# Overlapping the chunks of a conformer/attention residual block: the next chunk's input norm, GLU, q/k/v, convolution and its norm run inside this chunk's back half

## The chip, the cores and the metric

The kernel runs on one core of a Trainium2 chip. The metric is device time in microseconds for one launch, the median over several runs. All times below are microseconds unless they are marked ns.

## What is computed

One encoder layer over a stream of 2048 tokens with 1024 features, everything in float32:

```python
u = rms_norm(h, g_pre_mix); z = u @ w_in          # -> GLU input | q | k | v | branch gates
c = a * sigmoid(b)                                # a, b: the two halves of the GLU input
c = causal_depthwise_conv(c, conv_dw_w, conv_dw_b)    # 31 taps, 512 channels
c = silu(layer_norm(c)); y_conv = c @ w_conv_out
y_attn = sliding_window_sink_attention(rope(q), rope(k), v) @ w_attn_out   # 128-token window
h = h + rms_norm((sig(gA)*y_conv + sig(gB)*y_attn) @ w_out, g_post_mix)
gate, val = split(rms_norm(h, g_pre_ffn) @ w_up)  # 2 x 2816
gate = causal_depthwise_conv(gate, 3 taps)
h = h + rms_norm((gelu(gate) * val) @ w_down, g_post_ffn)
h = h + (p @ w_ple) * sigmoid(h @ w_ple_gate)
```

## The kernel before

The 2048 tokens are worked off in four chunks of 512 (chunk 0 to chunk 3). Features lie on the partitions, in tiles of 128 features by 512 tokens. Every operand of a large product is split into a high and a low part, and each 128x128 weight tile meets a 512-token tile in three matmuls (hi·hi, hi·lo, lo·hi). The weights are a stream of 122 blocks a chunk; a block holds 8 weight tiles, so it is 24 matmuls. Three slots hold blocks: SyncE loads block n as soon as block n-3 is done. In chunk 0 a block comes as float32 (0.5 MB), ScalarE and GpSimd split it, and both parts (1 MB) are stored to memory; in chunks 1 to 3 the two parts are loaded (1 MB).

Each engine runs one program, written out by hand; semaphores tie them together, and what stands first in an engine's program runs first. A chunk goes through these stages:

1. x is loaded and turned to feature-major by 32 TensorE transposes (L741); its norm gives `u_hi`, `u_lo`. This starts when the chunk ahead has ended.
2. GLU (8 blocks), then q and k with their rotation (`rope`, 5 blocks), then v as 96 matmuls of 128 columns (L760 to L762). VectorE runs the 31 x 4 taps of the convolution (L1069) during these and during attention.
3. Attention in four steps, each with two blocks of gate A between its small matmuls.
4. The layer norm of the convolution (mean L834, squares, `token_sums` L724, `spread` L731, which broadcasts a norm's factor over the partitions), and the merge of both branches (16 blocks).
5. `w_out` (8 blocks): `out_projection` on ScalarE squares and copies each result tile out of PSUM (L367, L524). Then the norm of its result (POST), the residual, and the pre-FFN norm (PRE), whose factor is not applied to `y_hi`/`y_lo` but later, to the up-projection's results (`r_ffn`).
6. The feed-forward in two parts: 16 tiles up (32 blocks), down (16 blocks); 6 tiles up (12), down (6). The first matmuls run four result banks at a time, and two more blocks go to banks 4 and 5 before a bank must be free again.
7. The norm of the feed-forward (PF) is taken while TensorE runs the `w_ple` blocks (2). Then `w_ple_gate` (8 blocks) needs `h3_hi`/`h3_lo`, the tiles of h after the residual; the result is turned back and stored.

A norm over the features is a chain: the last square (ScalarE), its sum (VectorE), `token_sums` (TensorE), the root (ScalarE), six small steps and `diag` (VectorE), `spread` (TensorE).

Of the kernel before, what the change touches and what calls it, by code (L numbers as in the profile page):

```python
# [15 lines left out]
P = 128  # L29
# [12 lines left out]
TAPS_A, TAPS_B = 6, 10  # L42
# [7 lines left out]
F1 = 16  # L50
F2 = NF - F1
# [12 lines left out]
B_UP1 = B_WO + KD_  # L64
B_DN1 = B_UP1 + 2 * F1
B_UP2 = B_DN1 + 2 * KD_
B_DN2 = B_UP2 + 2 * F2
B_WP = B_DN2 + F2 * KD_ // 8
B_PG = B_WP + NP * KD_ // 8
NB = B_PG + KD_  # L70
assert NB == 122 and all(b % 2 == 0 for b in (B_QKV, B_GA, B_MRG, B_WO, B_UP1, B_DN1, B_UP2, B_DN2, B_WP, B_PG, NB))
# [16 lines left out]
N_X, N_LN, N_POST, N_PRE, N_PF = range(5)  # L88
NORMS = 5
Q_LN, Q_POST, Q_PRE, Q_PF = 0, NC, NC + KD_, NC + 2 * KD_  # L90
NQ = NC + 3 * KD_

# [9 lines left out]
def build_kernel(nc, x, p, positions, weights, columns, identity, split_weights, out):  # L102
    with ExitStack() as ctx:
# [1342 lines left out]
```

## Time and profile before

| | us |
|---|---|
| median of 3 runs | 3052.93 (3051.05 to 3054.32) |
| the profiled execution, its own time | 3054.54 |
| its span, first to last instruction | 3052.7 |
| TensorE busy in the span | 2903.9 (95%) |
| VectorE busy | 1564.0 (51%) |
| ScalarE busy | 920.4 (30%) |
| mean granted share of the TensorE clock | 0.973 |

The profiled execution lies 1.6 above the median; the span is 1.8 short of its own time. TensorE's matmuls are pipelined, so its 95% says only that it seldom stands still; how dense the work is has to be read from the distance between matmul starts. The chunks' `w_out` stages start at 325.72, 1087.78, 1825.24 and 2562.93.

### The profile page before, as it was taken

The numbers are of one execution on the slowest core, as the hardware profiler recorded it, in microseconds if no ns is written. First come the engines' busy times: TensorE is split into PE (matmuls) and PEld (weight loads), VectorE is DVE, ScalarE is ACT, GpSimd is POOL, SyncE is SP. The second block draws the span as 40 slices with busy tenths as digits, with TensorE's granted clock in tenths as the row PEclk, the third lists the DMA queues.
The fourth block names the chain that finished last, engine by engine and source line by source line (L and its number), as shares of the span: only waits on it lengthen the run. The fifth ranks groups of instructions, "written<-read, shape, count | busy, mean of one in ns | idle before, by whom it ended". The sixth has DMA issues, their size and how long they took to land.

```text
span 3052.7 us, 33514 instructions
## 1 busy us (share of the span) xinstructions
PE 2903.9 (95%) x13232; PEld 2401.6 (79%) x13232; DVE 1564.0 (51%) x2535; ACT 920.4 (30%) x1661; POOL 299.7 (10%) x126
## 2 busy tenths in 40 slices
PE   6888899999899999999999999999999999899998
PEld 5776778887788778888878887888887878788887
DVE  6894477325778426412458834540356862542035
ACT  3463343333426223111233522210123541311013
POOL 2223334444200000000000000000000000000000
PEclk8799999999999999999999999999999999999999
DMA  5445757877743454555454344455555345455555
GB/s 208 172 164 215 284 213 289 290 285 280 262 167 137 158 184 176 194 194 189 184 207 171 133 179 176 183 193 194 189 189 208 142 151 195 160 193 193 193 193 179
DMA packets 180925, 600.37 MB, mean 197 GB/s; under 512 B 18336, under 2 KB 37024, under 8 KB 180768
## 3 DMA queue, kind: packets, MB, share of 16 engines
q1 hardware_dynamic: 163872, 589.83, 53.0%
q10 hardware_dynamic: 16896, 8.39, 0.9%
q8 instruction: 105, 1.72, 0.2%
q14 instruction: 52, 0.43, 0.0%
HBM read 461.84 MB, written 136.31 MB: 196 GB/s over the span
## 4 chain that ended last, share of the span: by engine, by line
PE 79%; DVE 15%; ACT 3%; issue 2%; DMA 1%; POOL 0%; ACTq 0%; POOLq 0%; SPq 0%; DVEq 0%
PE ps L690 22%; PE ps L691 21%; PE ps L692 21%; DVE conv_acc L1069 7%; PE ps L711 4%; PE ps L712 4%; PE ps L715 4%; PE ps L731 1%; DVE prob L1151 1%; DVE s_max L1130 0%; POOL w_lo L318 0%; DVE ca_lo L1162 0%; DVE y_tmp L1205 0%; PE ps L724 0%; DVE h L1042 0%
## 5 line engine op out<-in xcount | busy, mean ns | idle before, releaser
L690 PE MATMUL ps<-y_hi,w_hi 128*128 128x512 f32 x1536 | 602.9, 392 | 7.8 <-POOL w_lo L318 5.2
L692 PE MATMUL ps<-y_hi,w_lo 128*128 128x512 f32 x1536 | 598.9, 390 | 0.0
L691 PE MATMUL ps<-y_lo,w_hi 128*128 128x512 f32 x1536 | 598.8, 390 | 0.0
L1069 DVE SCALAR_TENSOR_TENSOR conv_acc<-conv_in,col,conv_acc 128x512 f32<-128x512 f32 x480 | 350.9, 803 | 0.8
L318 POOL TENSOR_TENSOR w_lo<-w_stage,w_hi 128x1024 fp32r<-128x1024 f32 x122 | 299.5, 2456 | 515.5 <-ACT w_hi L356 515.5
L690 PEld LDWEIGHTS ps<-y_hi,w_hi 128*128 128x128 f32 x1536 | 289.1, 188 | 71.3 <-DVE f_val L1262 4.3
L692 PEld LDWEIGHTS ps<-y_hi,w_lo 128*128 128x128 f32 x1536 | 289.0, 188 | 60.6
L691 PEld LDWEIGHTS ps<-y_lo,w_hi 128*128 128x128 f32 x1536 | 289.2, 188 | 59.9 <-issue 1.0
L690 PE MATMUL ps<-u_hi,w_hi 128*128 128x512 f32 x800 | 320.9, 401 | 0.4 <-POOL w_lo L318 0.4
L691 PE MATMUL ps<-u_lo,w_hi 128*128 128x512 f32 x800 | 313.5, 392 | 0.0
L692 PE MATMUL ps<-u_hi,w_lo 128*128 128x512 f32 x800 | 313.4, 392 | 0.0
L690 PE MATMUL ps<-f_hi,w_hi 128*128 128x512 f32 x768 | 301.5, 393 | 2.2 <-DVE f_lo L1283 2.2
L691 PE MATMUL ps<-f_lo,w_hi 128*128 128x512 f32 x768 | 299.5, 390 | 0.0
L692 PE MATMUL ps<-f_hi,w_lo 128*128 128x512 f32 x768 | 299.5, 390 | 0.0
L356 ACT ACTIVATE w_hi<-w_stage 128x1024 fp32r<-128x1024 f32 x122 | 129.1, 1059 | 267.2 <-PE ps L692 214.4
L1293 DVE TENSOR_TENSOR f_lo<-ps,f_hi 128x512 fp32r<-128x512 f32 x8 | 5.2, 686 | 339.9 <-ACT f_hi L597 339.9
L690 PEld LDWEIGHTS ps<-u_hi,w_hi 128*128 128x128 f32 x800 | 152.0, 190 | 34.1 <-issue 3.4
L691 PEld LDWEIGHTS ps<-u_lo,w_hi 128*128 128x128 f32 x800 | 151.9, 190 | 33.5 <-issue 3.0
L692 PEld LDWEIGHTS ps<-u_hi,w_lo 128*128 128x128 f32 x800 | 151.5, 189 | 32.1
L711 PE MATMUL ps<-y_hi,w_hi 128*128 128x512 f32 x384 | 154.5, 402 | 17.8 <-ACT y_hi L548 9.9
L690 PEld LDWEIGHTS ps<-f_hi,w_hi 128*128 128x128 f32 x768 | 144.6, 188 | 33.4 <-DVE f_lo L1283 2.6
L691 PEld LDWEIGHTS ps<-f_lo,w_hi 128*128 128x128 f32 x768 | 144.5, 188 | 30.6 <-issue 1.0
(179 smaller groups left out, 3991.9 us busy)
## 6 DMA issues: line engine op xcount, KB each, us to landing
w_hi<-split_weights SPq DMA_DIRECT2D x366, 512.0 KB, 3.2
w_lo<-split_weights SPq DMA_DIRECT2D x366, 512.0 KB, 4.2
w_stage<-in_weights SPq DMA_DIRECT2D x122, 512.0 KB, 4.3
split_weights<-w_hi SPq DMA_DIRECT2D x122, 512.0 KB, 2.6
split_weights<-w_lo SPq DMA_DIRECT2D x122, 512.0 KB, 3.9
x_rows<-in_x SPq DMA_DIRECT2D x5, 2048.0 KB, 10.2
out_h<-ple ACTq DMA_DIRECT2D x32, 256.0 KB, 5.2
p_rows<-in_p SPq DMA_DIRECT2D x4, 512.0 KB, 5.9
```

Source lines behind the costliest of these rows:

```text
L318: nc.gpsimd.tensor_tensor(w_lo[:, b % SLOTS], w_stage[:, b % SLOTS], w_hi[:, b % SLOTS].bitcast(F32), ALU.subtract).then_inc(w_lo_ready, 1)
L356: copy(w_hi[:, b % SLOTS], w_stage[:, b % SLOTS], ACT.Copy).then_inc(w_hi_ready, 1)
L690: nc.tensor.matmul(bank, w_hi[:, slot, kk], hi, start=start, stop=False)
L691: nc.tensor.matmul(bank, w_hi[:, slot, kk], lo, start=False, stop=False)
L692: return nc.tensor.matmul(bank, w_lo[:, slot, kk], hi, start=False, stop=stop)
L711: nc.tensor.matmul(ps[:, banks[o]], w_hi[:, slot, first + o], hi[:, k], start=(k == 0), stop=False)
L712: nc.tensor.matmul(ps[:, banks[o]], w_lo[:, slot, first + o], hi[:, k], start=False, stop=False)
L715: last = nc.tensor.matmul(ps[:, banks[o]], w_hi[:, slot, first + o], lo[:, k], start=False, stop=(k == 7))
L731: nc.tensor.matmul(ps[:, BC], ones[:, :], diag[:, :, :].rearrange("p t n -> p (t n)"), start=True, stop=True).then_inc(bc_ready, 1)
L1069: V.scalar_tensor_tensor(dst, src, column("conv_w", t + j * TAPS), dst, ALU.mult, ALU.add).then_inc(conv_tap, 1)
L1151: V.tensor_tensor(prob[:, s], prob[:, s], s_rec[:, s].unsqueeze(2).broadcast_to([P, PAIRS, P]), ALU.mult).then_inc(pn_ready, 1)
L1293: V.tensor_tensor(f_lo[:, F1 - NP + k], ps[:, PV + k], f_hi[:, F1 - NP + k].bitcast(F32), ALU.subtract).then_inc(p_lo, 1)
```

## The change

The order of the blocks across chunks is now a list that all engines read:

```python
order = [(0, b) for b in range(B_GLU, B_GA)]
for c in range(CHUNKS):
    order += [(c, b) for b in range(B_GA, B_UP[0])]
    if c + 1 < CHUNKS:
        order += [(c + 1, b) for b in range(B_GLU, B_QKV)]
    order += [(c, b) for b in range(B_UP[0], B_WP)]
    if c + 1 < CHUNKS:
        order += [(c + 1, b) for b in range(B_QKV, B_GA)]
    order += [(c, B_PG + j) for j in range(4)]
    order += [(c, b) for b in (B_WP, B_PG + 4, B_PG + 5, B_WP + 1, B_PG + 6, B_PG + 7)]
```

So chunk c+1's GLU (8 blocks) stands between chunk c's `w_out` and its up-projection, and chunk c+1's q, k, v (6 blocks) between chunk c's last down-projection and its `w_ple_gate`. The 122 blocks a chunk are the same ones. With them move:

- x is loaded twice: `rows_u` (four loads of 0.5 MB, issued before block 2 of `w_out`) is scaled row by row by its norm and turned for `u_hi`/`u_lo`; `rows_h` (2 MB, issued before block 3 of `w_out`) is turned for h. Both turnings stand inside `w_out`'s blocks 4 to 7, 16 tiles in all, through banks 0 and 2, so that block 4 first waits until `out_projection` has emptied these two.
- v is a whole block of 24 matmuls like the others, followed by four transposes.
- The taps of the next chunk's convolution stand in VectorE's program in groups of two inside the up-projection's tiles (42 of them in each of the first two parts), and 40 more beside the first down-projection.
- The feed-forward has three blocks of 8, 8 and 6 tiles; the PRE factor is applied to the input (`u2_tile`), not to the results; the conv over the gate reads PSUM.
- Output tiles are turned back and stored in the next chunk's attention.
- The layer norm of the next chunk's convolution stands between the `w_ple_gate` blocks.

TensorE's program after `w_out` (condensed; `more` is false in chunk 3, where all `c + 1` parts drop out):

```diff
+                if more:
+                    pe.wait_ge(y2_out, c * KD_ + 6)
+                    glu_pair(c + 1, 0, between=lambda: token_sums(POST, c))
+                    spread(POST, c)
+                    glu_pair(c + 1, 1)
+                    glu_pair(c + 1, 2)
+                    token_sums(PRE, c)
+                    glu_pair(c + 1, 3, between=lambda: spread(PRE, c))
+                else:
+                    token_sums(POST, c)
+                    spread(POST, c)
+                    token_sums(PRE, c)
+                    spread(PRE, c)
+                by_tile(c, B_UP[0], UP_BANK[0] + UP_BANK[1], y_hi, y_lo, u2_hi, u2_lo, c * KD_)
+                for t in range(2, FB[1]):
+                    up(c, t)                      # waits ft_ready >= c * NF + t - 1
...
+                down(c, 2)
+                if more:
+                    full_block(c + 1, B_QKV, QK_BANK[0], u_hi, u_lo)
+                token_sums(PF, c)
+                if more:
+                    full_block(c + 1, B_QKV + 1, QK_BANK[1], u_hi, u_lo)
+                spread(PF, c)
+                if more:
+                    for j in range(2, PAIRS + 1):
+                        full_block(c + 1, B_QKV + j, QK_BANK[j], u_hi, u_lo)
+                    full_block(c + 1, B_QKV + PAIRS + 1, V_BANK, u_hi, u_lo)
+                    pe.wait_ge(rope_done, (c + 1) * (PAIRS + 1) + 4)
+                by_tile(c, B_PG, PG_BANK[0:4], y_hi, y_lo, h3_hi, h3_lo, c * KD_,
+                        between=(lambda: value_rows(c + 1)) if more else None)
+                ple_tiles(c, 0)
+                if more:
+                    conv_mean(c + 1)
+                ple_gate(c, 4)
+                if more:
+                    token_sums(LN, c + 1)
+                ple_gate(c, 5)
+                if more:
+                    spread(LN, c + 1)
+                ple_tiles(c, 4)                   # tile j waits ple_mul of tile j - 2
```

On VectorE, at the place after the norm PF, the program before has this (h_tmp and h are the residual, y_lo the low part that `w_ple_gate` needs):

```order
L1227 TENSOR_TENSOR h<-h,h_tmp 128x512
L1320 TENSOR_TENSOR y_lo<-h,y_hi 128x512
L1222 SCALAR_TENSOR_TENSOR h_tmp<-acc,col,ps 128x512
L1227 TENSOR_TENSOR h<-h,h_tmp 128x512
L1320 TENSOR_TENSOR y_lo<-h,y_hi 128x512
L1222 SCALAR_TENSOR_TENSOR h_tmp<-acc,col,ps 128x512
L1227 TENSOR_TENSOR h<-h,h_tmp 128x512
```

The changed program has the rotation of the next chunk's q (rope_a, rope_b, qT) among them:

```order
L1365 SCALAR_TENSOR_TENSOR h_tmp<-acc,col,ps 128x512
L1370 TENSOR_TENSOR h<-h,h_tmp 128x512
L1365 SCALAR_TENSOR_TENSOR h_tmp<-acc,col,ps 128x512
L1370 TENSOR_TENSOR h<-h,h_tmp 128x512
L1431 TENSOR_TENSOR y_lo<-h,y_hi 128x512
L1246 TENSOR_TENSOR rope_a<-ps,cos_t 128x512
L1247 TENSOR_TENSOR rope_b<-rope_b,sin_t 128x512
L1250 TENSOR_TENSOR qT<-rope_a,rope_b 128x512
L1431 TENSOR_TENSOR y_lo<-h,y_hi 128x512
```

This group of nine stands three times in a row, once for each of the q tiles 1 to 3; what moved in are the three rotation steps.

On ScalarE, at the same place, the program before makes the copies y_hi one after the other:

```order
L342 ACT_TABLE_LOAD
L342 ACTIVATE n_root<-ps,col 128x4
L615 ACTIVATE ple<-ps 128x512 x6
L619 ACTIVATE y_hi<-h 128x512 x8
L629 ACTIVATE ple<-ps 128x512 x2
```

The changed program has the swapping copies of the rotation (four of 32 partitions for each q or k tile) between them:

```order
L430 ACT_TABLE_LOAD
L430 ACTIVATE n_root<-ps,col 128x4
L471 ACTIVATE rope_b<-ps 32x512 x4
L597 ACTIVATE y_hi<-h 128x512 x3
L471 ACTIVATE rope_b<-ps 32x512 x4
L597 ACTIVATE y_hi<-h 128x512 x2
L471 ACTIVATE rope_b<-ps 32x512 x4
```

Each swap now stands behind a y_hi copy that waits for VectorE's residual, and VectorE's rope_a waits for the swap.

On VectorE, around the squares of the layer norm, before:

```order
L1179 SCALAR_TENSOR_TENSOR conv_acc<-ps,conv_acc 128x512 x4
L1030 MEMSET ssum 128x512
L1036 TENSOR_TENSOR ssum<-ssum,sq 128x512 x4
L987 TENSOR_SCALAR n_var<-ps 128x4
L988 RECIPROCAL n_r<-n_root 128x4
```

and in the changed program, between `w_ple_gate`'s blocks:

```order
L1324 SCALAR_TENSOR_TENSOR conv_acc<-ps,conv_acc 128x512 x4
L1153 MEMSET ssum 128x512
L1442 TENSOR_TENSOR ple_t<-ps,ple_sg 128x512
L1444 TENSOR_TENSOR h<-h,ple_t 128x512
L1442 TENSOR_TENSOR ple_t<-ps,ple_sg 128x512
L1444 TENSOR_TENSOR h<-h,ple_t 128x512
L1160 TENSOR_TENSOR ssum<-ssum,sq 128x512 x4
```

Two tiles of the per-layer embedding (`ple_add`) now stand between the centring and the sums of the squares.

## Rows read from the trace of the kernel before

**Rows 1.** The page, busy time by engine: us, share, instructions.

```profile
PE 2903.9 (95%) x13232; PEld 2401.6 (79%) x13232; DVE 1564.0 (51%) x2535; ACT 920.4 (30%) x1661; POOL 299.7 (10%) x126
```

**Rows 2.** Windows: stretch, length, busy and count by engine, clock, DMA share, GB/s.

```profile
1320.85:1407.90 87.05, 87.05 (x386) 72.03 (x384) 2.08 (x3) 5.46 (x9) 0.00 (x0) 1.00 0.53 193
...
325.72:1087.78 762.06, 727.00 (x3309) 598.98 (x3308) 447.06 (x628) 279.73 (x465) 200.94 (x83) 0.98 0.65 234
1087.78:1825.24 737.46, 716.84 (x3308) 593.83 (x3307) 351.15 (x628) 197.94 (x382) 0.00 (x0) 0.99 0.50 181
2562.93:3052.74 489.81, 471.19 (x2087) 387.62 (x2085) 182.36 (x322) 106.58 (x168) 0.00 (x0) 0.98 0.51 186
```

**Rows 3.** Windows, as above: places in chunk 1 where TensorE is less dense.

```profile
914.45:925.12 10.67, 10.67 (x98) 10.67 (x96) 8.59 (x13) 3.97 (x8) 0.00 (x0) 1.00 0.27 100
990.70:1022.38 31.68, 26.57 (x111) 20.51 (x110) 21.81 (x40) 11.02 (x19) 0.00 (x0) 0.95 0.32 117
1109.54:1142.15 32.61, 25.02 (x107) 19.33 (x106) 10.01 (x20) 10.78 (x20) 0.00 (x0) 0.91 0.51 185
1510.81:1521.36 10.55, 8.77 (x41) 6.75 (x40) 5.07 (x13) 4.08 (x9) 0.00 (x0) 1.00 0.36 125
1566.79:1579.32 12.53, 6.97 (x52) 5.44 (x50) 9.30 (x20) 7.42 (x13) 0.00 (x0) 0.90 0.61 184
...
1142.15:1146.66 4.51, 4.51 (x11) 3.54 (x12) 4.51 (x8) 1.95 (x4) 0.00 (x0) 0.50 0.01 4
1142.15:1320.85 178.70, 178.41 (x778) 146.96 (x779) 89.38 (x161) 43.28 (x64) 0.00 (x0) 0.99 0.50 183
```

**Rows 4.** Timeline, norm POST of chunk 1: start, length, engine, instruction, idle before.

```profile
1132.18 0.69 DVE L1036 TENSOR_TENSOR ssum<-ssum,sq 128x512 f32<-128x512 f32 x1 [4.58 <-ACT sq L367]
1133.02 1.02 PE L724 MATMUL ps<-ones,ssum 128*128 128x1 f32 x8 [1.56 <-DVE ssum L1036]
1134.13 1.28 ACT L342 ACT_TABLE_LOAD   x1 [1.54 <-PE ps L724]
1135.42 0.26 ACT L342 ACTIVATE n_root<-ps,col 128x4 f32<-128x4 f32 x1
...
1137.61 2.07 PE L731 MATMUL ps<-diag,ones 128*128 128x512 f32 x2 [3.56 <-DVE diag L998]
...
1139.72 0.75 DVE L1222 SCALAR_TENSOR_TENSOR h_tmp<-acc,col,ps 128x512 f32<-128x512 f32 x1 [1.62 <-PE ps L731]
1140.50 0.69 DVE L1227 TENSOR_TENSOR h<-h,h_tmp 128x512 f32<-128x512 f32 x1
...
1141.29 0.72 ACT L548 ACTIVATE y_hi<-h,col 128x512 fp32r<-128x512 f32 x1 [5.60 <-DVE h L1227]
...
1142.15 0.77 PE L711 MATMUL ps<-y_hi,w_hi 128*128 128x512 f32 x1 [2.47 <-ACT y_hi L548]
```

**Rows 5.** Timeline, ScalarE: out-projection tiles 0 and 1 of chunk 1.

```profile
1110.23 0.60 ACT L367 ACTIVATE sq<-ps 128x512 f32<-128x512 f32 x1 [15.93 <-PE ps L715]
...
1111.68 0.62 ACT L524 ACTIVATE acc<-ps 128x512 f32<-128x512 f32 x1
```

**Rows 6.** Window, as in Rows 2: x and weights loaded together.

```profile
1550.00:1562.00 12.00, 12.00 (x62) 10.11 (x62) 5.67 (x9) 3.26 (x6) 0.00 (x0) 1.00 0.99 370
```

**Rows 7.** Groups by line, VectorE: instruction, count, busy, mean ns, idle before.

```profile
L1069 DVE SCALAR_TENSOR_TENSOR conv_acc<-conv_in,col,conv_acc 128x512 f32<-128x512 f32 x480 | 350.9, 803 | 0.8
```

**Rows 8.** Timeline, ScalarE and VectorE: one rotation in chunk 1.

```profile
909.26 2.40 ACT L409 ACTIVATE rope_b<-ps 32x512 f32<-32x512 f32 x4 [3.04 <-PE ps L692]
...
910.24 0.68 DVE L1101 TENSOR_TENSOR rope_a<-ps,cos_t 128x512 f32<-128x512 f32 x1
...
911.55 0.69 DVE L1105 TENSOR_TENSOR qT<-rope_a,rope_b 128x512 f32<-128x512 f32 x1
```

**Rows 9.** Timeline, VectorE: layer norm of chunk 1.

```profile
1004.08 2.48 DVE L1179 SCALAR_TENSOR_TENSOR conv_acc<-ps,conv_acc 128x512 f32<-128x512 f32 x4 [1.62 <-PE ps L834]
...
1007.14 1.52 DVE L1036 TENSOR_TENSOR ssum<-ssum,sq 128x512 f32<-128x512 f32 x2
```

More of the change, by code:

```diff
@@ new lines, in gate_b_tile, with centred_squares, silu @@
+            def gate_b_tile(c, j):
+                done(c, GB_BLOCK[j])
+                if j >= 2:
+                    act.wait_ge(merged, c * KD_ + j - 1)
+                copy(gate_b[:, j % 2], ps[:, GB_BANK[j % 2]], ACT.Sigmoid).then_inc(gate_b_ready, 1)
+            def centred_squares(c, first, end):
+                for j in range(first, end):
+                    act.wait_ge(ln_centred, c * NC + j + 1)
+                    square(LN, c, j, conv_acc[:, j], j % 2)
+            def silu(c, first, end):
+                for j in range(first, end):
@@ new lines, in product, with full_block @@
+            def product(bank, c, b, kk, hi, lo, start, stop):
+                slot = PLACE[c, b] % SLOTS
+                nc.tensor.matmul(bank, w_hi[:, slot, kk], hi, start=start, stop=False)
+                nc.tensor.matmul(bank, w_hi[:, slot, kk], lo, start=False, stop=False)
+                return nc.tensor.matmul(bank, w_lo[:, slot, kk], hi, start=False, stop=stop)
+            def full_block(c, b, bank, hi, lo, between=None):
+                ready(c, b)
+                for k in range(8):
+                    if k == 4 and between is not None:
+                        between()
+                    last = product(ps[:, bank], c, b, k, hi[:, k], lo[:, k], k == 0, k == 7)
+                last.then_inc(block_done, 1)
@@ new lines, in token_sums, with spread @@
+            def token_sums(kind, c):
+                pe.wait_ge(ss_added, c * NQ + Q_AT[kind] + (NC if kind == LN else KD_) + 2)
+                for t in range(TT):
+                    last = nc.tensor.matmul(ps[:, SMALL, t:t + 1], ssum[:, P * t:P * t + P], ones[:, 0:1],
+                                            start=True, stop=True)
+                last.then_inc(ssum_done, 1)
+            def spread(kind, c):
+                pe.wait_ge(diag_ready, c * 4 + kind + 1)
+                nc.tensor.matmul(ps[:, BC], ones[:, :], diag[:, :, :].rearrange("p t n -> p (t n)"),
+                                 start=True, stop=True).then_inc(bc_ready, 1)
@@ L967, in _ @@
+                ple_gate(c, 7)
+                if not more:
+                    for f in range(2, KD_):
+                        out_tile(c, f, 6 + f % 2)
         @block.vector
@@ new lines, in add_down, with h3_tile @@
+            def add_down(c, q, j):
+                if q == 1:
+                    dve.wait_ge(dn_first, c * KD_ + j + 1)
+                else:
+                    dve.wait_ge(dn_acc, c * 2 * KD_ + j + 1)
+                done(c, dn_done(q, j))
+                V.tensor_tensor(acc[:, j], acc[:, j], ps[:, dn_bank(q, j)], ALU.add).then_inc(dn_acc, 1)
+            def h3_tile(c, j):
+                if j >= 2:
+                    dve.wait_ge(h3_mid, c * KD_ + j - 1)
+                normed(c, j, "g_post_ffn", h3_step)
+                residual(c, j, h3_step, h3_mid)
```

2042 lines of the change are left out of this document (1098 added, 944 removed).

## Prediction

> **What bounds the kernel now.** The page's busy times come first [rows 1]: TensorE 95%, VectorE 51%, ScalarE 30%. TensorE sets the end, so I read the rest as one question: how much of its time is not dense matmul? The densest stretch gives the unit. 384 matmuls of the first down-projection take 87.05 [rows 2], 0.2267 each, so a block of 24 is 5.44. A chunk's 122 blocks are 663.8. A steady chunk, from one `w_out` to the next, takes 737.5 [rows 2]: 73.7 is something else. Chunk 0 (weights split on the fly) takes 762.1 for the same stretch, and the last one has 489.8 from `w_out` to the end. The windows then show where the 73.7 lies [rows 3]: v's 96 small matmuls take 10.67 for what a block does in 5.44; the layer norm's stretch holds four blocks (21.8) and lasts 31.7; the stretch of the norm POST again holds four blocks and lasts 32.6; the norm PF's holds 30 matmuls (6.8) and lasts 10.6; the chunk boundary holds only transposes and a broadcast and lasts 12.5.
>
> The timeline [rows 4] shows what such a gap is: the last sum at 1132.18, `token_sums`, table load 1.28, root and `diag` to 1137.61, then residual and copy, and TensorE starts again at 1142.15. It starts slow: for the next 4.51 the granted clock is 0.50 [rows 3], the 1.2 GHz level, and some ten matmuls run where twenty would at 2.4 GHz. So this gap costs about 2.2 more than its length.
>
> **What goes, in a steady chunk.** v as a block and four transposes: 10.67 - 5.44 - 0.4 = 4.8. The boundary: 12.5, plus 2.1 for the slow start, less 1.6 for four output tiles that only move: 13.0. Layer norm: 31.7 - 21.8 = 9.9, of which its sums and broadcasts (2.1) stay: 7.8. POST: 32.6 - 21.8 = 10.8; the stretch behind it, with PRE's sums and factor, holds 768 matmuls (174.1) in 178.7 [rows 3], 4.6 more; 15.4 in all, of which four small steps, 2.9, stay: 12.5. PF: 10.6 - 6.8 - 1.4 = 2.3. Together **40.4**.
>
> **What comes, in a steady chunk.** Most of the moved work is covered: for taps, six at 0.66 to 0.80 [rows 7] plus some 3.5 of its own is under the 10.9 that TensorE needs for an up tile. But I walked the order of each engine and found places where TensorE catches up.
> - *Turning x twice.* 16 tiles where there were 8, and they now cut into blocks. A tile's four transposes are about 0.4 and a break 0.05: 7.1.
> - *Banks 0 and 2.* `w_out` block 4 waits until two result tiles are squared and copied: from 1109.54, the end of the four-bank part, to 1112.3 [rows 5]: 2.8.
> - *Loads.* From the end of the merge, x (2 + 2 MB) goes ahead of `w_out`'s block 3. With blocks 2 and 3 that is 6.3e6 bytes; at the 370 GB/s of a full queue [rows 6] 17 plus a latency of about 2 gives 19, and block 3 is wanted after three blocks, 16.3. I take 3; bounds 0 and 8.
> - *Third up tile.* Before, two blocks went to banks 4 and 5 here. Now `up(2)` waits for tile 0's `f_tmp`: tap on ScalarE 0.6, two on VectorE 0.75 each, two conv taps 1.3, product 0.7, hand-overs: 4.5, plus 2.1: 6.6. Without cover nothing else hides it. Bounds 3.5 and 7.
> - *Rotation before `w_ple_gate`.* TensorE needs rotations 0 to 3 done. A group of nine VectorE instructions waits in its middle: two residual tiles 2.8 (pitch 1.39, from 0.78 and 0.61 [rows 4]), ScalarE's copy of the second 0.65, its swap 2.40 [rows 8], then rope 1.95 and a low part 0.6: 8.5, where VectorE's own work is 6.0. From the broadcast of PF: 1.06 + first tile and rotation 3.9 + two groups 17 + the third up to its rotation 8.0 = 29.9; TensorE has the broadcast 0.55 and four blocks 21.8, that is 22.3. Wait 7.6, plus 2.1: 9.7. Bounds 0 (VectorE never waits for the swaps) and 11.
> - *Layer norm's sums.* One block covers centring 2.6 (with 0.9 to start), zeroing 0.5, two embedding tiles 2.8, and four sums that alternate with squares 3.0 [rows 9]: 9.6 against 5.4. Wait 4.1, plus 2.1: 6.2. Bounds 2 and 7.
> - *Embedding tiles 6 and 7.* Tile 6 waits for scaling 2.6 and a product; tile 7 for two silus, a table load 1.28 and a sigmoid on ScalarE: 1.3 + 1.4 = 2.7. Bounds 0 and 5.
>
> Together **38.1**. A steady chunk changes by -2.3.
>
> The Trainium skill has a rule against this change: a switch of the activation table is a load of about 1283 ns and a drain, about 2.66 us together (ScalarE: Activation LUTs, What ACT_TABLE_LOAD costs). The changed kernel alternates sigmoid, silu and root between the `w_ple_gate` blocks. In the trace the load is 1.28 and the root starts 0.01 later, so no drain is seen; by the skill's figure tile 7 would wait 1.4 longer in each of three chunks, and the sum would be 4 higher.
>
> **The first chunk.** Up to `w_out` I expect nothing. The taps bind there: VectorE's 62 or so [rows 7] times 0.8 and more between GLU and scores, so v's shorter time is not the end's; and ScalarE splits three weight blocks before it copies the first tile of x. Bounds -5 and +4. From there to chunk 1's `w_out`: -2.3, its longer boundary gone too (4), but the x loads meet 1.5 MB of weight traffic a block, and block 3's split comes after them: +8. So +2; bounds -6 and +10.
>
> **The last chunk** has no next chunk to cover anything. Banks 2.8, h's eight tiles 3.6. POST and PRE stand bare: the chain to the first sum 2.5, 3.3 from sums to broadcast (4.6 in rows 4 less the table load, which runs ahead now), 2.1 to VectorE, then eight tiles of normed, residual and sum, 0.66 + 0.6 + 0.6 and a start, 16.4; sums to broadcast 3.3; tile and copy 3.2; with ends 31.0, slow start 2.2. That is 33.2 against the 15.4 of now: 17.8. Third up tile 5.8. PF: 9.5 + 2.1 against 3.9: 7.7. The tail 0.5. Together **38.2**.
>
> **Sum.** 0 + 2 - 2 x 2.3 + 38.2 = +35.6 on the profiled execution's own 3054.5, so 3090; the median of before lies 1.6 lower, and I round down a little, to **3086**, since the 2.1 of a slow start need not follow a wait as short as some of these. Dropping the slow starts at the new waits takes 22 away, the loads 9, the first chunk 9 more at its low bound; loads at 8 and the first chunk at its high bound add 25. Range 3054 to 3112.
>
> **Rivals.**
> 1. *The hand-overs don't bind* (faster). If VectorE keeps its own pace between residual and rotation and between centring and squares, the group of nine is 6.0, rotations end at 34 just with TensorE, the layer norm's wait shrinks to what its own sums need and the embedding tiles are free: 18.6 less in each of three chunks, 3086 - 56 = 3030. It decides from some 13 saved a chunk. For it: VectorE is only half busy, and an out-of-step copy can be done early. Against it: ScalarE runs its list in order, and the swap stands behind a copy that waits. Chance 0.12.
> 2. *The loads starve TensorE*: 4 MB of x at the worst place; if a wait of 8 with a slow start follows in chunks 1 and 2 and 20 in chunk 0, +26: 3112. For it: the queue is at 0.99 with 2 MB [rows 6]. Against it: steady chunks load at half of what it can. Chance 0.15.
> 3. *It cancels*: my forecast with no slow starts after new waits and cheaper loads, 3050 to 3058. Chance 0.13.
> The forecast itself, 3058 to 3104: 0.60.
>
> A measurement of this kernel tells about 0.2%, 6, from no change. Faster by more: rival 1 and a little of 3, 0.13. Within: 0.09. Slower: 0.78.
>
> **What would show it.** `w_out` to `w_out` in the steady chunks 733 to 738, and 525 to 532 from the last `w_out` to the end. TensorE waits of 7 to 8 before `w_ple_gate` on the rotation, 4 to 5 before the third up tile on the product, 4 before the layer norm's sums, and one of some 20 in the last chunk before the PRE sums. If steady chunks take under 725, rival 1 holds and the forecast is wrong; if `w_out`'s blocks 2 and 3 wait over 5 for weights, rival 2.

## The result and the profile after

The changed kernel takes 3161.9 (3159.15 to 3165.26, four runs) against 3053.62 of the kernel before (3051.05 to 3055.86, four runs): the ratio is 1.0355, interval 1.0337 to 1.0373. That is 108 slower, where 33 was forecast, and outside the range.

The page of the changed kernel has TensorE and ScalarE busy within 7 of [rows 1], VectorE 154 less, and a span that is 105 longer:

```profile
span 3157.3 us, 32749 instructions
...
PE 2910.3 (92%) x13080; PEld 2397.9 (76%) x13080; DVE 1410.4 (45%) x2392; ACT 917.1 (29%) x1635; POOL 322.9 (10%) x126
```

So the 105 are not more work: they are waits, and matmuls at a lower clock (the mean granted clock is 0.963 in this execution, 0.973 before). GpSimd's 322.9 for the same 126 instructions, against 299.7, points to one of the causes; I come to it below. The windows, cut at the start of each chunk's `w_out` (length, busy of PE, PEld, DVE, ACT and POOL, clock, DMA share, GB/s), say where the waits are. They answer to [rows 2]:

```profile
0.00:328.44 328.44, 256.46 (x1152) 211.58 (x1153) 213.97 (x315) 141.46 (x267) 101.90 (x43) 0.93 0.54 194
328.44:1147.45 819.01, 732.28 (x3272) 602.06 (x3271) 389.66 (x596) 281.12 (x462) 221.03 (x83) 0.95 0.61 221
1147.45:1887.82 740.37, 718.57 (x3272) 594.70 (x3270) 324.27 (x596) 199.51 (x379) 0.00 (x0) 0.98 0.50 183
1887.82:2627.62 739.80, 718.14 (x3272) 593.84 (x3270) 324.29 (x596) 199.52 (x379) 0.00 (x0) 0.98 0.50 183
2627.62:3157.34 529.72, 484.89 (x2119) 395.74 (x2117) 158.20 (x289) 95.53 (x149) 0.00 (x0) 0.95 0.47 172
```

| stretch | before | after | difference | forecast |
|---|---|---|---|---|
| start to `w_out` of chunk 0 | 325.7 | 328.4 | +2.7 | 0 |
| to `w_out` of chunk 1 | 762.1 | 819.0 | +56.9 | +2 |
| to `w_out` of chunk 2 | 737.5 | 740.4 | +2.9 | -2.3 |
| to `w_out` of chunk 3 | 737.7 | 739.8 | +2.1 | -2.3 |
| to the end | 489.8 | 529.7 | +39.9 | +38.2 |

The last chunk is as forecast, the steady ones are 5 dearer each, and the first is wrong by 55. TensorE's chain of waits over that stretch (line, what it waited for: total, times, longest) names the reason:

```profile
PE ps L741 <- POOL w_lo L403: 41.0, 6, 20.5
PE ps L765 <- POOL w_lo L403: 16.0, 4, 7.5
PE ps L765 <- issue: 13.4, 1, 13.4
PE ps L741 <- DVE f_tmp L1408: 5.8, 1, 5.8
```

57.0 are waits for GpSimd's `w_lo`, the low part of a weight block that is split in chunk 0 only. The same view of the kernel before has 6.0, 0.8 of them in `w_out` and these:

```profile
PE ps L690 <- POOL w_lo L318: 5.2, 3, 2.3
```

The 13.4 "issue" is in part of the same kind: ScalarE's split for the first `w_ple_gate` block starts at 903.87, behind its copies, and GpSimd's part ends just before TensorE starts at 907.42.

The steady chunk shows the hand-overs that the prediction walked through, one by one:

```profile
PE ps L765 <- DVE qT L1250: 7.4, 1, 7.4
PE ps L741 <- DVE f_tmp L1408: 4.0, 1, 4.0
PE ps L778 <- DVE ssum L1160: 3.3, 1, 3.3
PE ps L765 <- DMA w_lo<-split_weights: 3.0, 1, 3.0
PE ps L741 <- issue: 2.2, 1, 2.2
PE ps L741 <- DVE ple_t L1442: 1.8, 2, 1.1
```

So there are three questions. Why does GpSimd come late in chunk 0, although its own work is unchanged? Do the steady waits cost what the forecast put on them, and can they go? And does the overlap pay when they are gone?

**The longest wait, 20.5.** The timelines of GpSimd and of VectorE around it (start, length, engine, instruction, idle before):

```profile
562.82 23.49 POOL L403 TENSOR_TENSOR w_lo<-w_stage,w_hi 128x1024 fp32r<-128x1024 f32 x2 [14.35 <-ACT w_hi L422]
```

```profile
555.20 26.58 DVE L1208 SCALAR_TENSOR_TENSOR conv_acc<-conv_in,col,conv_acc 128x512 f32<-128x512 f32 x40
```

```profile
584.13 0.76 PE L741 MATMUL ps<-f_hi,w_hi 128*128 128x512 f32 x1 [20.46 <-POOL w_lo L403]
```

Two splits take 23.49. The view by tile (count: shortest, median and longest in ns) gives the longer of them:

```profile
L403 POOL TENSOR_TENSOR w_lo<-w_stage,w_hi x5: 2355/2387/21167, 546.1 to 597.8; 128x1024 fp32r<-128x1024 f32 x5
```

One split takes 21.2 and the others 2.4. The long one begins while the 40 taps run, which fill 555.20 to 581.78 with no gap between two, and ends 2.2 behind the last of them: about the 2.4 that a split takes alone. So it stood for the rest of the row, 19.0, and then ran. No weight is missing; SyncE can't store the block, and so can't load the next, before this split is done. It goes the other way too, for one instruction at a time: here a VectorE step of a kind that takes 0.43 beside it takes 2.55, from just behind GpSimd's start to just behind its end.

```profile
542.58 2.34 POOL L403 TENSOR_TENSOR w_lo<-w_stage,w_hi 128x1024 fp32r<-128x1024 f32 x1 [4.39 <-ACT w_hi L422]
542.65 2.55 DVE L1182 TENSOR_SCALAR angle<-angle,col 128x512 f32<-128x512 f32 x1
```

The Trainium skill has the rule for this (SBUF — State Buffer, Who interferes with whom): VectorE and GpSimd share a pair of ports as an exclusive lock, held for a whole instruction, and a VectorE instruction with two inputs in SBUF contends with a GpSimd instruction that reads SBUF. A tap has two such inputs. The two rows above show the whole-instruction lock, but their VectorE step has only one tensor as input. The kernel before shows it with two inputs; in its steady chunk this product takes 0.69:

```profile
505.06 2.40 POOL L318 TENSOR_TENSOR w_lo<-w_stage,w_hi 128x1024 fp32r<-128x1024 f32 x1 [3.05 <-ACT w_hi L356]
505.60 2.40 DVE L1281 TENSOR_TENSOR f_tmp<-g_act,f_val 128x512 f32<-128x512 f32 x1 [0.99 <-ACT g_act L576]
```

By the rule as it stands a split waits for one tap, 0.66; here it waits for what is left of a row of them. My prediction didn't weigh this rule.

A row of taps need not do that, though. At the start of chunk 0 the same trace has a row of 28, and five splits arrive in it:

```profile
62.11 29.33 DVE L1208 SCALAR_TENSOR_TENSOR conv_acc<-conv_in,col,conv_acc 128x512 f32<-128x512 f32 x28
```

```profile
L403 POOL TENSOR_TENSOR w_lo<-w_stage,w_hi x5: 2406/2481/2987, 64.3 to 85.8; 128x1024 fp32r<-128x1024 f32 x5
```

None takes over 3.0, as the rule has it. These 28 taps alternate between two tiles of `conv_acc`, and each waits for the last but one; the 40 go round four tiles. A row of 16 over four tiles in the kernel before shows both cases, and it was there to be read before the prediction:

```profile
213.73 12.79 DVE L1069 SCALAR_TENSOR_TENSOR conv_acc<-conv_in,col,conv_acc 128x512 f32<-128x512 f32 x16
```

```profile
214.51 2.85 POOL L318 TENSOR_TENSOR w_lo<-w_stage,w_hi 128x1024 fp32r<-128x1024 f32 x1 [2.67 <-ACT w_hi L356]
223.68 5.04 POOL L318 TENSOR_TENSOR w_lo<-w_stage,w_hi 128x1024 fp32r<-128x1024 f32 x1 [6.32 <-ACT w_hi L356]
```

The split that comes 0.8 behind the row's start gets in; the one that comes 10 behind it ends 2.2 after the row's last tap (226.52). What decides between the two cases no run here tests.

### The profile page after: what moved, and what is told of

It reads as the page before. It is cut to its first block, busy times and chain, and to the rows that moved or that the text cites. A ratio compares the mean times of both kernels' runs of the same rounds, so it can differ in the third digit from the quotient of the medians.

```text
span 3157.3 us, 32749 instructions
## 1 busy us (share of the span) xinstructions
PE 2910.3 (92%) x13080; PEld 2397.9 (76%) x13080; DVE 1410.4 (45%) x2392; ACT 917.1 (29%) x1635; POOL 322.9 (10%) x126
## 4 chain that ended last, share of the span: by engine, by line
PE 78%; DVE 5%; DMA 2%; ACT 2%; POOL 1%; issue 1%; SPq 0%; DVEq 0%; ACTq 0%
PE ps L741 21%; PE ps L742 21%; PE ps L743 21%; PE ps L765 4%; PE ps L766 4%; PE ps L769 3%; POOL w_lo L403 1%; DMA w_stage<-in_weights 1%; PE ps L790 1%; DMA w_lo<-split_weights 1%; PE ps L876 1%; ACT rope_b L471 1%; DVE h L1370 1%; DVE h_tmp L1365 1%; PE ps L778 1%
## 5 line engine op out<-in xcount | busy, mean ns | idle before, releaser
L741 PE MATMUL ps<-y_hi,w_hi 128*128 128x512 f32 x1536 | 612.5, 399 | 31.4 <-DVE f_tmp L1408 17.8
L403 POOL TENSOR_TENSOR w_lo<-w_stage,w_hi 128x1024 fp32r<-128x1024 f32 x122 | 322.7, 2649 | 660.4 <-ACT w_hi L422 660.4
L1208 DVE SCALAR_TENSOR_TENSOR conv_acc<-conv_in,col,conv_acc 128x512 f32<-128x512 f32 x480 | 387.1, 865 | 0.1
L741 PEld LDWEIGHTS ps<-y_hi,w_hi 128*128 128x128 f32 x1536 | 293.6, 191 | 96.5 <-DVE f_tmp L1408 19.5
L741 PE MATMUL ps<-u_hi,w_hi 128*128 128x512 f32 x704 | 280.5, 398 | 4.1 <-POOL w_lo L403 4.1
L743 PE MATMUL ps<-u_hi,w_lo 128*128 128x512 f32 x704 | 275.6, 391 | 0.0
L742 PE MATMUL ps<-u_lo,w_hi 128*128 128x512 f32 x704 | 275.3, 391 | 0.0
L1398 DVE SCALAR_TENSOR_TENSOR g_conv<-ps,col,g_conv 128x511 f32<-128x511 f32 x88 | 65.9, 749 | 388.8 <-ACT g_conv L583 388.6
L765 PE MATMUL ps<-y_hi,w_hi 128*128 128x512 f32 x384 | 159.7, 416 | 53.7 <-POOL w_lo L403 16.0
L743 PEld LDWEIGHTS ps<-f_hi,w_lo 128*128 128x128 f32 x768 | 146.1, 190 | 31.0
L741 PEld LDWEIGHTS ps<-u_hi,w_hi 128*128 128x128 f32 x704 | 133.3, 189 | 33.6 <-issue 5.4
L1421 DVE TENSOR_TENSOR acc<-acc,ps 128x512 f32<-128x512 f32 x64 | 43.9, 687 | 257.0 <-PE ps L743 257.0
```

What stands on the lines that cost most here:

```text
L403: nc.gpsimd.tensor_tensor(w_lo[:, slot], w_stage[:, slot], w_hi[:, slot].bitcast(F32), ALU.subtract).then_inc(w_lo_ready, 1)
L741: nc.tensor.matmul(bank, w_hi[:, slot, kk], hi, start=start, stop=False)
L742: nc.tensor.matmul(bank, w_hi[:, slot, kk], lo, start=False, stop=False)
L743: return nc.tensor.matmul(bank, w_lo[:, slot, kk], hi, start=False, stop=stop)
L765: nc.tensor.matmul(ps[:, banks[o]], w_hi[:, slot, first + o], hi[:, k], start=(k == 0), stop=False)
L1208: V.scalar_tensor_tensor(dst, src, column("conv_w", t + j * TAPS), dst, ALU.mult, ALU.add).then_inc(conv_tap, 1)
```

## Experiments

The stretches of each kernel, from its profiled execution, cut as above; medians and ratios beside them. The kernel before ran beside each group: 3051.04 with e1 to e4, 3052.39 with e5 to e8, 3053.0 with e9 to e11, 3053.45 with e12. A stretch comes from one execution and carries some 3 of its own: one that the edit doesn't touch reads 736.9 for 739.8 (e2, chunk 2 to 3) and 532.9 for 529.7 (e6, the last). In e2's case block 3's load is waited for twice, at most 2.0 each, where the change has one wait of 2.6, and the granted clock is 0.99 for 0.98.

| kernel | chunk 0 to 1 | 1 to 2 | 2 to 3 | 3 to end | median | ratio, interval |
|---|---|---|---|---|---|---|
| the change | 819.0 | 740.4 | 739.8 | 529.7 | 3161.9 | 1.0355, 1.0337 to 1.0373 |
| e1 breaks | 802.2 | 740.4 | 740.7 | 531.2 | 3145.11 | 1.0309, 1.0286 to 1.0332 |
| e2 taps later | 805.6 | 740.5 | 736.9 | 531.5 | 3148.06 | 1.0315, 1.0293 to 1.0338 |
| e3 columns | 799.0 | 736.9 | 740.6 | 528.8 | 3129.76 | 1.0253, 1.0225 to 1.0281 |
| e4 swap first | 812.3 | 730.0 | 727.5 | 531.3 | 3136.65 | 1.0281, 1.0266 to 1.0296 |
| e5 split first | 808.9 | 740.4 | 739.8 | 529.7 | 3150.92 | 1.0326, 1.0311 to 1.0341 |
| e6 squares first | 820.7 | 735.2 | 733.8 | 532.9 | 3153.4 | 1.0332, 1.0315 to 1.035 |
| e7 banks | 819.3 | 733.4 | 733.9 | 524.7 | 3144.14 | 1.0303, 1.0288 to 1.0319 |
| e8 load order | 822.1 | 732.7 | 734.5 | 531.5 | 3154.24 | 1.0337, 1.0321 to 1.0352 |
| e10 splits | 764.0 | 740.3 | 740.6 | 528.8 | 3106.67 | 1.0179, 1.0163 to 1.0194 |
| e11 hand-overs | 810.9 | 710.2 | 710.6 | 523.5 | 3087.99 | 1.0114, 1.0099 to 1.0129 |
| e9 all | 757.8 | 709.6 | 709.4 | 521.7 | 3024.5 | 0.9904, 0.9888 to 0.9921 |
| e12 later breaks | 750.5 | 709.7 | 709.4 | 522.1 | 3024.94 | 0.9911, 0.9894 to 0.9927 |

### e1 and e2: the row of 40 taps

e1, on VectorE:

```diff
-                    taps(40)
+                    for k in range(5):
+                        taps(8)
+                        if c == 0 and k < 4:
+                            dve.wait_ge(w_lo_ready, FRESH[PLACE[c, B_DN[0] + 3 + k]])
```

> Chunk 0 of the changed kernel has one TensorE wait of 20.6 in the first down-projection, on GpSimd's w_lo (L403): two splits took 23.5 there, where one takes 2.4, while VectorE ran 40 taps of the next chunk's convolution without a break. Here VectorE waits, in chunk 0 alone, after every eighth tap until GpSimd has made one more w_lo; the work is the same. Theory (an unbroken row of taps keeps GpSimd from starting): the wait goes, and with it about 4 of slow clock: 3138. Rival (the loads of chunk 0 come late, whoever computes): the wait stays and the time is 3160 or more.

e2, on VectorE:

```diff
-                    taps(40)
+                    if c:
+                        taps(40)
...
                 for t in range(FB[2], FB[3]):
-                    up(c, t)
+                    up(c, t, (3, 3, 2) if c == 0 and t + 1 < FB[3] else (0, 0, 0))
```

> In chunk 0 alone the 40 taps leave the first down-projection and stand in threes and twos inside the up tiles of the third part. Theory (unbroken taps keep GpSimd from starting): 3138, as with the breaks, and GpSimd's splits in the third part stay under 5 each. Rival (chunk 0 has more VectorE work than GpSimd's splits can live with, wherever it stands): the wait moves to the third part and the time stays above 3155.

The view by tile again, for the same stretch, of e1 and then of e2:

```profile
L403 POOL TENSOR_TENSOR w_lo<-w_stage,w_hi x9: 2360/2706/2769, 546.4 to 598.0; 128x1024 fp32r<-128x1024 f32 x9
...
  PE ps L741: 1.7, 1
```

```profile
L403 POOL TENSOR_TENSOR w_lo<-w_stage,w_hi x9: 2353/2392/2574, 546.5 to 598.1; 128x1024 fp32r<-128x1024 f32 x9
...
  PE ps L741: 1.8, 1
```

In 52 GpSimd makes nine splits where it made five; none takes over 2.8, and the wait of 20.5 is 1.7. In e1 VectorE does the same taps in the same place, so the rival (late loads) and the rival of e2 (too much VectorE work) both fall. The breaks don't work by ending the row early enough: e1's split at 566.95 comes 1.3 behind the start of a row of 8 (565.65; such a row alone lasts 5.4) and takes 2.41, where being held to the row's end would make it some 6. It gets in, as at the start of the 16. Both runs are slower than the 3138 expected. The stretch is 16.8 and 13.4 shorter, not 24: between the first and the second down-projection e1 wins 19.5 (141.6 for 161.1), and some 3 come back in small pieces later; in e2 the waits for `w_lo` from 600 on are 4 longer than in the change (19.8 for 15.5).

### e3: one weight block at the start of a down-projection, not two

```diff
-                ready(c, B_DN[q])
-                ready(c, B_DN[q] + 1)
-                for k in range(count):
...
+                for j in range(2):
+                    for k in range(count):
+                        if (count * j + k) % 8 == 0:
+                            ready(c, B_DN[q] + (count * j + k) // 8)
```

> Each down-projection does its output column 0 whole and then column 1, where it alternated between them; so it needs one weight block at its start, not two. In chunk 0 TensorE waits 5.4 before each of the three down-projections, for the second block's w_lo, whose split stands on ScalarE behind the last tile's f_hi. Theory: these three waits go, 15.6: 3146; chunks 1 to 3 change by less than 1 each. Rival (the wait is for the last tile's f_lo): one column covers 4.8 (in the third part 3.4) where two covered twice as much, so nothing is gained in chunk 0 and up to 2 a down-projection is lost in all: 3162 to 3180.

The three waits are gone, without one for `f_lo` in their place: the stretch falls by 20.0, three waits of 5.0 to 5.4 and their slow clock. The cause is the order on ScalarE. Its list for an up tile is tap, gelu, f_hi, and the last two wait for VectorE; the split of the second down block stood behind all three. The median fell by 32, more than the profile of one execution accounts for; its four runs lie between 3116.53 and 3135.27, wider than those of most kernels here. Its profiled execution accounts for 24 (spans 3157.3 and 3133.2): the 20.0 (15.6 was expected) and 3.5 in chunk 1 to 2, no more than a stretch carries of its own. 8 of the median's 32 stay open.

### e4: the swap ahead of the copies

```diff
                 for j in range(1, PAIRS):
+                    if more:
+                        rope_swap(c + 1, j)
                     h3_tile(c, 2 * j - 1)
                     h3_tile(c, 2 * j)
-                    if more:
-                        rope_swap(c + 1, j)
```

> ScalarE makes the rotation's swapping copies ahead of the two y_hi copies that stood before them, nothing else. Theory (the group of nine VectorE instructions waits for the swap, and the swap for a copy that waits for VectorE): VectorE's idle 2.6 per group goes, the wait of 7.5 before w_ple_gate and its 1.9 of slow clock go in chunks 1 and 2, and 7.5 of the 13.8 in chunk 0: 3136. Rival (VectorE's own work, 6.0 a group, sets it): under 5 in all, 3157 to 3162.

3136.65, as expected. In the changed kernel VectorE stands still in each group of nine, for the swap; e.g. in chunk 1:

```profile
1641.55 0.69 DVE L1431 TENSOR_TENSOR y_lo<-h,y_hi 128x512 fp32r<-128x512 f32 x1
1644.81 0.69 DVE L1246 TENSOR_TENSOR rope_a<-ps,cos_t 128x512 f32<-128x512 f32 x1 [2.58 <-ACT rope_b L471]
```

With the swap first, TensorE's wait for `qT` is no more among the waits of a steady chunk, which is 10.4 and 12.3 shorter. So the forecast's 9.7 for this interlock was right, and so was its bound of 11 nearly. In chunk 0 it is 6.7: the split behind it takes over.

### e5: splits ahead of ScalarE's other waits

```diff
+                split_until(PLACE[c, B_PG])
                 h3_tile(c, 7)
                 if more:
+                    split_until(PLACE[c, B_PG + 1])
                     rope_swap(c + 1, PAIRS)
...
                 copy(v_feat[:, :], ps[:, V_BANK], ACT.Copy).then_inc(v_out, 1)
+                if c:
+                    split_until(PLACE[c - 1, B_PG + 3])
```

> ScalarE's w_hi copies (splits) for the first four w_ple_gate blocks of chunk 0 stand earlier in its list: those of blocks 0 and 1 around the last y_hi copy, ahead of the last swap, those of blocks 2 and 3 ahead of its wait for v's four transposes. Nothing else changes. Theory (in chunk 0 TensorE waits for splits that stand behind ScalarE's own waits; for blocks 2 and 3 ScalarE waits for transposes that TensorE makes only after 48 matmuls): of the 13.8 before w_ple_gate 4.6 go, the 7.7 behind the transposes go, with some slow clock 13 to 14: 3148. Rival (the loads are late): 3160.

10.2 off the stretch from chunk 0 to 1, where 13 to 14 was expected, and nothing elsewhere. The timeline of ScalarE in the changed kernel shows the circle that it cuts:

```profile
908.42 0.60 ACT L477 ACTIVATE v_feat<-ps 128x512 f32<-128x512 f32 x1
920.44 0.31 ACT L480 ACTIVATE v_even<-v_even 64x128 f32<-64x128 f32 x1 [11.42 <-PE ps L820]
...
924.33 2.00 ACT L422 ACTIVATE w_hi<-w_stage 128x1024 fp32r<-128x1024 f32 x2
```

ScalarE waits 11.4 for v's transposes, which TensorE makes only after 48 matmuls of `w_ple_gate`; the blocks that TensorE needs after the transposes are split only at 924.33.

### e6: the layer norm's squares first

```diff
-                    centred_squares(c + 1, 0, 2)
+                    centred_squares(c + 1, 0, NC)
                 ple_gate(c, 2)
                 ple_gate(c, 3)
                 if more:
-                    centred_squares(c + 1, 2, NC)
                     sum_root(LN, c + 1, CONV)
```

and on VectorE `ln_squares` ahead of `ple_add(c, 2)`.

> ScalarE's squares and VectorE's sums of the layer norm stand ahead of embedding tiles 2 and 3, in all of chunks 0 to 2. Theory (the sums wait for two embedding tiles, 2.8): 2.5 of the wait of 3.5 before the sums go, and some 1.5 of slow clock, three times: 3150. Rival (the norm's small steps now wait behind those tiles, so its broadcast comes as late as before): 3158 to 3164.

5.2 and 6.0 less in the steady chunks, near the 6.2 that the forecast had put there; in chunk 0 nothing: there the wait before these sums falls too, from 3.3 to 0.8, but those for `w_lo` rise from 57.0 to 58.9.

### e7: the third up tile on other banks

```diff
+        def up_bank(t, half):
+            return (4, 5)[half] if t == 2 else UP_BANK[t % 2][half]
...
-                pe.wait_ge(ft_ready, c * NF + t - 1)
+                if t > 2:
+                    pe.wait_ge(ft_ready, c * NF + t - 1)
+                elif c + 1 < CHUNKS:
+                    pe.wait_ge(glu_done, (c + 1) * NC + 4)
```

> The third up tile of each chunk writes banks 4 and 5 and need not wait for the first tile's f_tmp. Theory (a bank must come free, and nothing covers its chain): the waits of 5.8, 4.2, 4.2 and 4.1 go, each with up to 2.8 of slow clock: 25 to 28 less, 3135. Rival (the wait moves to the fourth tile): under 8 in all, 3154 or more.

7.0, 5.9 and 5.0 in chunks 1 to 3 (forecast 6.6, 6.6 and 5.8), and nothing in chunk 0, so 18 in place of 25: there the fourth tile now waits 4.5 for a split, the rival's case in this one chunk. The median, 3144.14, lies between the theory's 3135 and the rival's 3154.

### e8: rows_h behind block 3

```diff
-                if b == B_WO + SLOTS:
+                if b == B_WO + SLOTS + 1:
                     sp.dma_start(rows_h[:, :, :], rows_of(c)).then_inc(xh_loaded, 16)
```

> rows_h (2 MB) is issued behind w_out's block 3, not ahead of it. Theory (4 MB of x ahead of a block that is wanted after 16): TensorE's wait of 3.1 for block 3 goes in chunks 1 and 2, and most of 4.8 and 2.0 in chunk 0, each with slow clock: some 5 a chunk, 3147. Rival (the 2 MB of rows_u alone are enough to make it late, or the wait moves to block 4 and the transposes): 3158 to 3162.

7.7 and 5.3 less in the steady chunks, more than the 5 expected. In chunk 1 the wait itself was 3.0. Behind it the clock was low twice: 0.79 over the next 7.1, and 0.83 over the 10.0 behind the wait for banks that follows (2.2). In e8 the same wait for banks is still 2.2, but the 10.0 behind it have 1.00. The windows, of the change and then of e8:

```profile
1176.21:1186.21 10.00, 10.00 (x45) 8.27 (x46) 2.93 (x5) 4.37 (x9) 0.00 (x0) 0.83 0.24 83
```

```profile
1178.03:1188.03 10.00, 10.00 (x55) 8.47 (x56) 3.77 (x6) 5.20 (x10) 0.00 (x0) 1.00 0.41 152
```

The whole run is slower than the 3147 expected (3154.24), as chunk 0 is 3.1 longer: there one wait of 8.0 for banks takes the place of two, of 1.6 and 3.1: ScalarE splits a block whose load now stands behind rows_h, at 364.62, before it empties those banks.

```profile
367.72 0.76 PE L741 MATMUL ps<-y_hi,w_hi 128*128 128x512 f32 x1 [7.99 <-ACT acc L566]
```

### e10, e11 and e9: the splits, the hand-overs, and both

e10 holds e1, e3, e5 and two more early splits; e11 holds e4, e6, e7, e8 for chunks 1 to 3, and a bank wait that moves; e9 holds all ten. The new edits:

```diff
 # ScalarE, in up()
+                split_until(PLACE[c, up_block(t)] + SLOTS)
                 act.wait_ge(ft_ready, item)
 # ScalarE, among the u2 tiles
+                    if j == 5:
+                        split_until(PLACE[c, B_UP[0]] + SLOTS - 1)
+                split_until(PLACE[c, B_UP[0]] + SLOTS)
 # TensorE, w_out blocks 4 to 7
-                    pe.wait_ge(y2_out, c * KD_ + 2)
-
                     def turns(f):
+                        pe.wait_ge(y2_out, c * KD_ + 2)
```

> Only what concerns the splitting of weights, so chunk 0 alone: breaks in the 40 taps, column 0 of a down-projection whole before column 1, the splits for w_ple_gate earlier on ScalarE, and two more places where ScalarE splits a block before it waits for VectorE (among the pre-FFN input tiles, and before each up tile's f_tmp). The three edits that were tried singly took 16.8, 20.0 and 10.2 off the stretch from w_out of chunk 0 to w_out of chunk 1; the new two should take 3 to 6. Theory (all that chunk 0 lost beyond the other chunks is splits that come late): that stretch falls from 819 to about 767, near the 762 of the kernel before, and the time is 3110. Rival (the waits hide one another, and the stretch is bound by the sum of splitting and VectorE's work): it stays above 785, 3130.

> Only the hand-overs that every chunk has: swaps first, the layer norm's squares first, the third up tile on banks 4 and 5, rows_h behind block 3 (chunks 1 to 3), and a new one: w_out's block 4 starts at once and only the turning of x inside it waits for banks 0 and 2 (before, the whole block waited 2.6, four times). Theory (these waits are independent, and all the price of the overlap in a steady chunk): each steady chunk falls from 740 by 11 + 5.5 + 6.4 + 6.5 + 4 to about 707, the last one by 10, the first by 10 to 15: 3075 to 3085. Rival (VectorE is the next bound, so waits move to the next hand-over): steady chunks above 718, time above 3105.

> All ten edits together. Theory: chunk 0 to chunk 1 some 745 to 755, steady chunks 707, the last from w_out to the end 516: 3015 to 3025, faster than both kernels. Rival (the edits of chunk 0 do not add to the others): above 3040. If it is above 3053, the overlap can't be made to pay by order alone.

Windows of e10 (chunks 0 and 1) and then of e11 (the same):

```profile
329.81:1093.85 764.04, 723.45 (x3272) 597.63 (x3270) 403.79 (x596) 283.70 (x462) 204.56 (x83) 0.97 0.65 236
1093.85:1834.18 740.33, 718.77 (x3271) 595.28 (x3270) 324.34 (x596) 199.62 (x379) 0.00 (x0) 0.98 0.50 183
```

```profile
329.80:1140.71 810.91, 733.21 (x3272) 602.13 (x3270) 393.10 (x596) 281.19 (x462) 221.44 (x83) 0.95 0.62 223
1140.71:1850.93 710.22, 707.42 (x3272) 587.03 (x3271) 323.85 (x596) 199.35 (x379) 0.00 (x0) 1.00 0.52 191
```

The two answers separate cleanly. e10 takes 55.0 off chunk 0, 16.8 + 20.0 + 10.2 of them by the three edits measured singly, which leaves 8.0 for the new ones if the three add up, and leaves chunk 1 as it was: with splits in time chunk 0 costs 764.0, where the kernel before has 762.1. e11 takes 30 off each steady chunk, and its granted clock goes from 0.98 to 1.00: of TensorE's waits in chunk 1 none over 1.1 is left. That is 710 where 707 was expected, and the time is 3087.99 for 3075 to 3085.

Together they give 3024.5, 0.96% faster than the kernel before, at the upper end of what was expected (chunk 0, 757.8, and the last stretch, 521.7, are longer than the 755 and 516 said). The stretches say where the overlap pays: against the kernel before, the two steady chunks are 28 shorter each and chunk 0 is 4 shorter, while the start is 5 longer and the last chunk, which has no next one to cover it, 32 longer. That leaves 24 (spans 3052.7 and 3028.8). No run gives the kernel before those of the edits that it could take too, so how much of the 24 is the overlap alone is not measured.

### e12: breaks one split later

```diff
-                            dve.wait_ge(w_lo_ready, FRESH[PLACE[c, B_DN[0] + 3 + k]])
+                            dve.wait_ge(w_lo_ready, FRESH[PLACE[c, B_DN[0] + 4 + k]])
```

> As the kernel with all ten edits, but each of VectorE's four waits among the 40 taps asks for one more split than there (in that kernel the splits run one block ahead, two of the waits were met already, 24 taps ran without a break, and one split took 14.2; TensorE waited 10.5). Theory (what holds GpSimd off is the length of the unbroken row): no row is longer than 8 taps (5.3), no split takes over 6, TensorE's wait goes with some 3 of slow clock: 3010 to 3014. Rival (the splits and the taps together are too much for these 43 us): the wait stays or moves to the next up tile, 3020 or more.

The profile of e9 has 24 taps in one row, and one split that takes 14.2 beside them (it ends 2.2 behind the row, at 575.13):

```profile
556.95 15.98 DVE L1219 SCALAR_TENSOR_TENSOR conv_acc<-conv_in,col,conv_acc 128x512 f32<-128x512 f32 x24
```

```profile
L406 POOL TENSOR_TENSOR w_lo<-w_stage,w_hi x5: 2368/2392/14231, 553.9 to 590.1; 128x1024 fp32r<-128x1024 f32 x5
```

In e12, with rows of 8:

```profile
L406 POOL TENSOR_TENSOR w_lo<-w_stage,w_hi x9: 2347/2675/2917, 547.6 to 598.2; 128x1024 fp32r<-128x1024 f32 x9
```

So a long row held a split off again, and in rows of 8 none was: 21.2 beside 40 taps, 14.2 beside 24, at most 2.9 beside 8. The theory's mark for the splits (none over 6) is met, its time is not: TensorE's wait there goes, one of 4.5 appears before a later up tile, as the rival said, and the stretch is 7.3 shorter in the profiled executions. The medians don't show it (3024.5 and 3024.94): the profiled execution of e9, 3030.58, is its slowest, that of e12, 3021.77, its fastest. The expected 3010 to 3014 is missed, and the rival's 3020 or more is what came. Whether e9's long row occurs in its other executions can't be told, as only one has a profile.

## Why the prediction was wrong

- **The first chunk: "-2.3, its longer boundary gone too (4), but the x loads meet 1.5 MB of weight traffic a block, and block 3's split comes after them: +8. So +2; bounds -6 and +10."** This step failed; the stretch took 56.9 more. The steady chunk was walked engine by engine and its result was carried over, with one item added for the loads. But in chunk 0 ScalarE and GpSimd also have every weight block in their lists, and a hand-over on ScalarE is there one behind which a split can stand. The runs give: the row of taps 16.8, the second down block behind `f_hi` 20.0, `w_ple_gate`'s splits 10.2, and what is left of e10's 55.0, 8.0, to early splits elsewhere. All but the first can be read from the order on ScalarE with the splits in it. The 40 taps were taken as covered, and by TensorE's work they are; what they cost is on the engine beside them, which the prediction didn't look at. With all four out, in e10, the stretch is 764.0.
- **The steady chunk: "-2.3".** It was +2.9 and +2.1. The terms one by one: rotation 9.7, by e4 10.4 and 12.3; layer norm's sums 6.2, by e6 5.2 and 6.0; third up tile 6.6, by e7 7.0 and 5.9: right. Loads 3, by e8 7.7 and 5.3: the mis-sized one. 3.0 was right for the wait, but nothing was added for the slow clock after it, as had been done for the others, nor for that behind the next wait, which goes with it (e8). These four account for most of the 5 that each chunk was off.
- **The last chunk: "38.2".** 39.9. The longest wait is that before the PRE sums, 15.5, where some 20 was said; the third up tile is 4.0 as in the others:

```profile
PE ps L778 <- DVE ssum L1160: 21.1, 3, 15.5
PE ps L785 <- DVE diag L1146: 6.5, 3, 2.2
PE ps L741 <- DVE f_tmp L1408: 4.0, 1, 4.0
```

- **Embedding tiles 2.7**: the waits for `ple_t` are 1.8 in a steady chunk.
- **Slow starts.** The forecast took "a little" off since a slow start need not follow a short wait. In chunk 1 it did follow the short ones: 0.79 over 7.1 behind the wait of 3.0, 0.71 over the 10.0 behind that of 4.0. Behind the wait of 2.2 it came in the changed kernel and not in e8.
- **Rivals.** None held. "The loads starve TensorE" has its mark, a wait over 5 for weights, not met: 4.4 in chunk 0 for `w_lo`, 3.0 from memory in chunk 1. "The hand-overs don't bind" is refuted by e4, e6 and e7: they did. Its price of 18.6 a chunk was about right for the three hand-overs that it named: e4 and e6 took 15.6 and 18.3 together off a steady chunk. The 30 of e11 hold the third up tile, the loads and the bank wait besides, which it didn't price. The case that came, splits of weights late in chunk 0, was no rival at all, and the range was drawn as if chunk 0 were known within 8.
- **Slips that change nothing.** Rival 1 has the rotations end "at 34 just with TensorE"; by the forecast's own terms it is about 22, beside TensorE's 22.3. The three cuts at the low end, 22, 9 and 9, lead to 3046 and not to 3054. The layer norm's items add up to 8.9, or 9.8 with the 0.9 to start, for 9.6.
- **The table load.** The forecast set the drain of the Trainium skill (ScalarE: Activation LUTs, What ACT_TABLE_LOAD costs) against a trace without one. The new loads between `w_ple_gate`'s blocks show none either; silu starts 0.02 after its load of 1.28:

```profile
976.18 1.28 ACT L554 ACT_TABLE_LOAD   x1
977.48 0.72 ACT L554 ACTIVATE silu_c<-conv_acc,col 128x512 f32<-128x512 f32 x1
```

## What to carry to other kernels

A pass that does one-time work (here the splitting of weights) is a kernel of its own: walk every engine's order through it again when blocks move, since a wait that costs an ordinary pass only its own length can cost this one a late split as well. Overlap makes in-order lists longer between a producer and its consumer; before calling it slower by nature, list the waits of a steady stretch and ask of each whether two neighbours in a list could change places. Five such edits turned 740 into 710; with five more for the splits, a kernel that was 3.5% slower is 1% faster. When work is "covered" on one engine, look also for who needs a gap in it, and in the old kernel's trace for a small case of it: one split of 5.04 among 2.4s was the sign here.

## What the runs showed of the hardware

- A GpSimd tensor operation that reads SBUF can be held off by a row of VectorE instructions with two SBUF inputs until the row ends: 21.2 beside 40 of them, 14.2 beside 24, 5.04 at the end of 16, each ending 2.2 behind the row. It need not be: at most 3.0 within 28 that alternate between two tiles, 2.85 at the start of the 16, at most 2.9 with breaks every 8. What decides is open. A VectorE instruction in its turn waits for one whole GpSimd operation (2.55 for 0.43, 2.40 for 0.69).
- A wait costs more than its length. The waits of e12's chunk 1 come to 2.8, none over 1.1, and its window (1078.78 to 1788.48) has a granted clock of 1.00, the 2.4 GHz level; those of the changed kernel's chunk 1, shown above, come to 21.7 at 0.98. Of the 30.7 between the two chunks 18.9 are the waits. The rest, 11.8, is the difference in TensorE's busy time for the same 3272 matmuls (718.57 and 706.79):

```profile
PE ps L751 <- DVE ple_t L1453: 1.7, 2, 1.1
PE ps L788 <- DVE ssum L1171: 0.8, 1, 0.8
PE ps L751 <- DMA w_lo<-split_weights: 0.3, 1, 0.3
```

```profile
1078.78:1788.48 709.70, 706.79 (x3272) 587.36 (x3270) 323.88 (x596) 199.32 (x379) 0.00 (x0) 1.00 0.53 191
```
